# Moving four pieces of a two-layer trunk's first layer: parameter loads, token matrices, the gate's way up, and four weight splits

## The chip, the cores and the metric

One Trainium2 chip, one core of it. The metric is device time in microseconds of one execution. TensorE (PE) multiplies, VectorE (DVE), ScalarE (ACT) and GpSimd (POOL) do the rest, SyncE (SP) issues DMAs. Each engine runs its own list of instructions in order and waits on semaphores.

## What is computed

A trunk of two residual layers over x (1 x 256 x 1024, float32), each followed by a squared-ReLU MLP (1024 to 4096 and back). Layer 1 mixes tokens with sparse attention and isn't touched. Layer 0, where the change lies, is RWKV-7 time mixing:

```python
dx = shift(x) - x
xr, xw, xk, xv, xa, xg = (x + dx * mu[i] for i in range(6))
r, k, v = xr @ W_r, xk @ W_k, xv @ W_v
w_log = -softplus(-(w0 + tanh(xw @ w1) @ w2)) - 0.5
decay = exp(-exp(w_log))
a = sigmoid(a0 + (xa @ a1) @ a2)
g = sigmoid(xg @ g1) @ g2                      # the gate; g1 is 1024 x 160, g2 is 160 x 1024
kk = heads(k * k_k) / norm;  k = k * (1 + (a - 1) * k_a)
S_t = S_{t-1} diag(w_t) + (S_{t-1} (-kk_t)) (kk_t a_t)^T + v_t k_t^T;  y_t = S_t r_t
out = ((groupnorm(y) + bonus) * g) @ w_out     # bonus = sum(r k r_k) v, a head at a time
```

## The kernel before

Activations lie features first: 128 partitions x 8 feature tiles (FT) x 256 tokens. Weights of the big products stream in units of 128 x 1024 (four contraction tiles x 256 output columns) through a ring of four slots. Each unit is loaded into `raw` by SP, split by ACT into a rounded high part `whi` (`split`, L1076) and by DVE into the rest `wlo` (`rest`, L1468); `ahead(u)` does so for unit u + 4. TensorE adds three products a tile: whi by xh, whi by xl, wlo by xh (L450 to L452). `linear8` runs a projection: four groups of two units, with `between(g)` called behind a group and `after_unit(u)` behind a unit. Everything is ordered by hand: each engine's list, with semaphores.

*Front.* SP loads x by tokens, constants, 14 small pieces of parameters (`prow`), `spread`, then the weight units. ACT sums squares of x (L1097) and takes the root; DVE takes its reciprocal (L1483) and scales the identity and the shift matrix by it (`tokmat`, L1488). TensorE transposes the parameters (L472), which DVE copies to `par` (L1479) ahead of the reciprocal; then it multiplies x by `tokmat` (L483 to L485), which normalizes, transposes and takes the token difference in one. ACT takes that out to `xd` two features a call (`xd_out`), DVE mixes (`mix_pair`, L1496), ACT rounds (`upper`, L1125), DVE makes the rest (`lower`, L1505).

*Projections r, k, v.* Between the groups of v lie small products: `between_v(0)` spreads the inverse norms of kk (16 contraction rows, L594), `between_v(1)` is the gate's way up (`g_up`, L575 with 128 rows and L576 with 32), `between_v(2)` the pair sums for the bonus (L603). ACT computes E1, E2, E3 (exponentials of the running decay), DVE the factors AR and BK, and behind v TensorE transposes BK (`b_k`, L613) and V (L625). ACT and DVE copy these to BKT and UV; POOL multiplies the bonus by V (L2035).

*Inversion.* Two pairs of two sets of triangular 64 x 64 matrices are inverted (L658, L667), each opened by ACT's copy `Lr`, two masks by POOL, and DVE's mask, transpose and sum (L1686 to L1691).

*Recurrence.* Four chunks c of 64 tokens (NCH). TensorE's list in a chunk: `xs_state`, `y_state`, `gn_mean(c-1)`, u (L805), `gn_var(c-1)`, state (L815), `y_values`, `xs_values(c+1)`, `gn_spread(c-1)` (L755). DVE's: copies XS (L1739), `gn_scale(c-2)`, copy UV, the state's update, `gn_rstd(c-1)` (L1720, L1722), which `gn_spread` waits for. ACT's: XS, squares and copy for the mean, UV, `gn_sqrt`, the two y copies (L1296), `gn_upper(c-2)`. POOL applies the gate and makes `yl`. Then comes the output projection o0; its first four units are split right behind v's last.

Of the kernel before, what the change touches and what calls it, by code (L numbers as in the profile page):

```python
# [15 lines left out]
HD = 64  # L16
H = D // HD
C = 64
NCH = T // C
# [83 lines left out]
def rwkv_nsa_trunk(nc, t, out):  # L103
# [56 lines left out]
    lup_g1 = place("lup_g1", [LG - P, D], off(9, 4 * D))  # L160
    hg0 = place("hg0", [P, T], misc + 128)
    hg1 = place("hg1", [LG - P, T], misc + 128 + 4 * T)
# [145 lines left out]
    def sem(name):  # L308
        if name not in sems:
            sems[name] = ctx.enter_context(nc.semaphore(name))  # L310
        return sems[name]

    with ctx:
# [10 lines left out]
        def _(sp):  # L324
# [4 lines left out]
            pr = sem("par_in")  # L329
            for i, n in enumerate(["mix_norm", "mlp_norm"]):  # L330
                sp.dma_start(prow[16 * i:16 * i + 16, 0, :], t[n].rearrange("a (k p) -> (a k) p", p=P)).then_inc(pr, 16)
            sp.dma_start(prow[32:80, 0, :], t["rwkv_mu"][0].rearrange("a (k p) -> (a k) p", p=P)).then_inc(pr, 16)
            for i, n in enumerate(["rwkv_w0", "rwkv_a0", "rwkv_k_k", "rwkv_k_a"]):
                sp.dma_start(prow[80 + 8 * i:88 + 8 * i, 0, :], t[n][0].rearrange("(k p) -> k p", p=P)).then_inc(pr, 16)
            sp.dma_start(prow[112:120, 0, :], t["rwkv_r_k"][0].rearrange("(k a) n -> k (a n)", a=2)).then_inc(pr, 16)
            sp.dma_start(prow[120:128, 0, :], t["rwkv_ln_w"][0].rearrange("(k p) -> k p", p=P)).then_inc(pr, 16)
            sp.dma_start(prow[0:8, 1, :], t["rwkv_ln_b"][0].rearrange("(k p) -> k p", p=P)).then_inc(pr, 16)
            for a in range(2):
                sp.dma_start(prow[8:9, 1, a * HD:(a + 1) * HD], t["nsa_q_norm"]).then_inc(pr, 16)
                sp.dma_start(prow[9:12, 1, a * HD:(a + 1) * HD], t["nsa_k_norm"][0]).then_inc(pr, 16)  # L340
# [25 lines left out]
            sp.dma_start(lup_g1[:, :], t["rwkv_g2"][0][P:LG, :]).then_inc(lo, 16)  # L366
# [52 lines left out]
        def _(pe):  # L419
# [146 lines left out]
            def g_up():  # L566

                pe.wait_ge(sem("kkn_used"), 1)
                for g in range(4):
                    if g >= 2:  # L570
                        pe.wait_ge(sem("up_out"), 16 + g - 1)
                    for m in range(2):
                        c0 = (2 * g + m) * P
                        o = ps[:, 4 + 2 * (g % 2) + m, 0:T]
                        mm(o, lup_g0[:, c0:c0 + P], hg0[:, :], start=True, stop=False)  # L575
                        last = mm(o, lup_g1[:, c0:c0 + P], hg1[:, :], start=False, stop=True)  # L576
                    last.then_inc(sem("up_pe"), 1)
# [9 lines left out]
            def between_v(g):  # L587

                if g == 0:
                    pe.wait_ge(sem("spread_in"), 16)  # L590
                    pe.wait_ge(sem("lora_act"), 3)
                    pe.wait_ge(sem("kk_inv"), 1)
                    for k in range(FT):
                        last = mm(ps[:, 4 + k // 2, (k % 2) * T:(k % 2 + 1) * T], hspread(k), kkr[:, 1, :],  # L594
                                  start=True, stop=True)
                    last.then_inc(sem("kk_pe"), 1)
                if g == 1:
                    g_up()
                if g == 2:
                    pe.wait_ge(sem("rk"), 1)  # L600
                    pe.wait_ge(sem("up_out"), 20)
                    for j in range(4):
                        last = mm(ps[:, 4 + j, :], cc("pair"), t11[:, 2 * j:2 * j + 2, :], start=True, stop=True)  # L603
                    last.then_inc(sem("kk_pe"), 1)

            linear8("v", xh[0], xl[0], "v", between_v)


# [8 lines left out]
            pe.wait_ge(sem("bk_ready"), 2)  # L617
            pe.wait_ge(sem("rk_copied"), 1)
            b_k(0)
            b_k(1)  # L620
# [437 lines left out]
        def _(act):  # L1058
# [33 lines left out]

            act.wait_ge(sem("eps_set"), 3)
# [43 lines left out]
            upper("r", 0, 0)  # L1137
            xd_out(2)
            upper("r", 0, 1)
            xd_out(3)  # L1140
            split(1)
# [60 lines left out]
            A(hg1[:, :], ps[0:LG - P, 5, 0:T], ACT.Sigmoid).then_inc(sem("lora_act"), 1)  # L1202
# [3 lines left out]
            act.wait_ge(sem("cs_ready"), 1)  # L1206
            A(E1[:, :, :], CSm[:, :, :], ACT.Exp, scale=-DECAY).then_inc(sem("e1_ready"), 1)
# [3 lines left out]
            act.wait_ge(sem("ex_ready"), 1)  # L1211
            A(E2[:, :, :], CSm[:, :, :], ACT.Exp, scale=DECAY).then_inc(sem("e2_ready"), 1)
            A(E3[:, :, :], Sg[:, :, :], ACT.Exp, scale=-DECAY).then_inc(sem("e3_ready"), 1)
            evac_of("v", V, 1)
            ahead(U0["v"] + 2)
            ahead(U0["v"] + 3)
            for g in range(4):
                act.wait_ge(sem("up_pe"), FT + g + 1)
                b = 4 + 2 * (g % 2)
                A(Gt[:, 2 * g:2 * g + 2, :], ps[:, b:b + 2, 0:T], ACT.Copy).then_inc(sem("up_out"), 1)  # L1220
            evac_of("v", V, 2)
            ahead(U0["v"] + 4)
            ahead(U0["v"] + 5)
            act.wait_ge(sem("kk_pe"), KK_PE["rk_sum"])
            A(t11[:, :, :].rearrange("p (b k) t -> p b (k t)", b=4), ps[:, 4:8, :], ACT.Copy).then_inc(sem("rk_copied"), 1)
            evac_of("v", V, 3)
            ahead(U0["v"] + 6)
            ahead(U0["v"] + 7)
# [7 lines left out]
            bkt_copy(0)  # L1236

# [44 lines left out]
            for c in range(NCH):  # L1282
                for half in range(2):
                    act.wait_ge(sem(f"xs_pe{half}"), c + 1)
                    if c == 0:
                        act.wait_ge(sem("u_zero"), 1)
                    A(XS[half][0:HD, :, 0, :], quarter(ps[0:HD, 3 * half, 0:GW]), ACT.Copy).then_inc(sem(f"x_even{half}"), 1)
                if c:
                    gn_square(c - 1)
                act.wait_ge(sem("u_pe0"), c + 1)  # L1290
                A(UV[0:HD, c, 0:512], ps[0:HD, 1, :], ACT.Copy).then_inc(sem("u_sb0"), 1)
                if c:
                    gn_sqrt(c - 1)
# [159 lines left out]
        def _(dve):  # L1453
# [24 lines left out]
            dve.wait_ge(sem("par_t"), 1)  # L1478
            v.tensor_copy(par[:, 0:NPAR], ps[:, 7, 0:NPAR]).then_inc(sem("par_r"), 1)  # L1479
            dve.wait_ge(sem("par_r"), 1)  # L1480

# [8 lines left out]
            v.tensor_scalar(lastcol[:, :], tokc[:, P:P + 2], tiny[:, 6:7], None, ALU.mult).then_inc(sem("tok_ready"), 1)  # L1490

# [50 lines left out]
            for n in range(4):  # L1542
                dve.wait_ge(sem("xd_out"), 2 * n + 2)
                mix_pair(0, mixd[0], n)
                if n == 2:
                    rest(1, 2)
                if n:
                    lower("r", 0, n - 1)
            lower("r", 0, 3)
# [58 lines left out]
            for k in range(FT):  # L1608
# [4 lines left out]
            dve.wait_ge(sem("kk_pe"), KK_PE["kk_spread"])  # L1613
            v.tensor_tensor(KK[:, :, :].rearrange("p (b k) t -> p b (k t)", b=4), KK[:, :, :].rearrange("p (b k) t -> p b (k t)", b=4),
                            ps[:, 4:8, :], ALU.mult).then_inc(sem("kkn_used"), 1)
# [7 lines left out]
            dve.wait_ge(sem("kkn_used"), 1)  # L1623
            v.tensor_tensor(Ai[:, :, :], KK[:, :, :], Ai[:, :, :], ALU.mult).then_inc(sem("b_ready"), 1)
            dve.wait_ge(sem("up_out"), 20)
            dve.wait_ge(sem("e2_ready"), 1)
            step(v.tensor_tensor(arv(BK, 1), ch(K), ch(E2), ALU.mult))
            dve.wait_ge(sem("b_ready"), 1)
            v.tensor_tensor(arv(BK, 0), ch(Ai), ch(E2), ALU.mult).then_inc(sem("bk_ready"), 1)
            ahead2("v", 2)  # L1630
            dve.wait_ge(sem("e1_ready"), 1)
            step(v.tensor_tensor(arv(AR, 1), ch(R), ch(E1), ALU.mult))
            step(v.tensor_copy(PC[:, :, :], E1[:, :, :].rearrange("p k (c n) -> p k c n", n=C)[:, :, :, C - 1]))
            settle()
            dve.sem_inc(sem("rk_done"), 1)
            dve.sem_inc(sem("bk_ready"), 1)
            dve.sem_inc(sem("ar_ready"), 1)
            dve.wait_ge(sem("e3_ready"), 1)
# [3 lines left out]
            ahead2("v", 4)  # L1642
            ahead2("v", 6)
            dve.wait_ge(sem("bk_ready"), 2)
# [89 lines left out]
            for c in range(NCH):  # L1734
# [385 lines left out]
```

## Time and profile before

| | us |
|---|---|
| median of three runs | 859.94 |
| lowest and highest | 853.4, 860.27 |
| the profiled execution | 860.52 |
| its span, first to last instruction | 858.6 |
| mean granted TensorE clock | 0.959 |

| engine | busy us | share of the span |
|---|---|---|
| TensorE | 801.3 | 93% |
| DVE | 540.4 | 63% |
| ACT | 378.6 | 44% |
| POOL | 71.0 | 8% |

The median is that of whole executions; the profile is of one of them, and its times count from its first instruction. In the lists of the trace the first number is the start in us, the second the busy time. PEclk is the share of the full TensorE clock that was granted; full speed is 2.4 GHz, 0.50 is 1.2 GHz. A float32 product leaves two records in the trace, one of the split kind one.

### The profile page before, as it was taken

The numbers are of one execution on the slowest core, as the hardware profiler recorded it, in microseconds if no ns is written. First come the engines' busy times: TensorE is split into PE (matmuls) and PEld (weight loads), VectorE is DVE, ScalarE is ACT, GpSimd is POOL, SyncE is SP. The second block draws the span as 40 slices with busy tenths as digits, with TensorE's granted clock in tenths as the row PEclk, the third lists the DMA queues.
The fourth block names the chain that finished last, engine by engine and source line by source line (L and its number), as shares of the span: only waits on it lengthen the run. The fifth ranks groups of instructions, "written<-read, shape, count | busy, mean of one in ns | idle before, by whom it ended". The sixth has DMA issues, their size and how long they took to land.

```text
span 858.6 us, 18088 instructions
## 1 busy us (share of the span) xinstructions
PE 801.3 (93%) x7567; PEld 735.3 (86%) x7567; DVE 540.4 (63%) x780; ACT 378.6 (44%) x581; POOL 71.0 (8%) x48
## 2 busy tenths in 40 slices
PE   5899997988886999999999999978989999999997
PEld 4898776888765999999999988864549999999997
DVE  2785868667443687775455784567955877764441
ACT  4666625121332544443444434356755544443331
POOL 0000003164031000000000010003420000000000
PEclk9999889789997999999999999968999999999999
DMA  7753114000000579866565534310003565666551
GB/s 243 221 173 124 50 50 141 10 3 3 3 2 2 171 209 232 227 191 207 178 192 177 170 121 120 119 57 2 1 2 113 170 188 173 189 198 194 174 171 49
DMA packets 109995, 107.62 MB, mean 125 GB/s; under 512 B 7224, under 2 KB 108992, under 8 KB 109936
## 3 DMA queue, kind: packets, MB, share of 16 engines
q1 hardware_dynamic: 109936, 106.77, 41.5%
q8 instruction: 45, 0.74, 0.4%
q14 instruction: 14, 0.11, 0.0%
HBM read 105.71 MB, written 1.05 MB: 124 GB/s over the span
## 4 chain that ended last, share of the span: by engine, by line
PE 84%; DVE 10%; issue 2%; ACT 2%; SPq 1%; POOL 0%; DMA 0%; ACTq 0%; DVEq 0%
PE ps L450 21%; PE ps L452 21%; PE ps L451 20%; PE ps L667 4%; DVE SB L1970 1%; DVE nmx L1974 1%; PE ps L1022 1%; DVE Gs L1660 1%; PE ps L805 1%; PE ps L562 1%; PE ps L887 1%; PE ps L1005 1%; PE ps L483 1%; PE ps L948 1%; ACT SB L1416 1%
## 5 line engine op out<-in xcount | busy, mean ns | idle before, releaser
L1468 DVE TENSOR_TENSOR wlo<-raw,whi 128x1024 fp32r<-128x1024 f32 x188 | 228.5, 1240 | 112.3 <-ACT whi L1076 110.9
L450 PE MATMUL ps<-xh,whi 128*128 128x256 f32 x896 | 257.1, 287 | 2.1 <-DVE xl L1505 2.1
L452 PE MATMUL ps<-xh,wlo 128*128 128x256 f32 x896 | 255.3, 285 | 0.0
L451 PE MATMUL ps<-xl,whi 128*128 128x256 f32 x896 | 255.1, 285 | 0.0
L1076 ACT ACTIVATE whi<-raw 128x1024 fp32r<-128x1024 f32 x124 | 130.0, 1058 | 154.6 <-PE ps L452 149.8
L450 PEld LDWEIGHTS ps<-xh,whi 128*128 128x128 f32 x896 | 171.5, 191 | 7.7 <-issue 6.8
L451 PEld LDWEIGHTS ps<-xl,whi 128*128 128x128 f32 x896 | 171.1, 191 | 0.3 <-issue 0.2
L452 PEld LDWEIGHTS ps<-xh,wlo 128*128 128x128 f32 x896 | 171.2, 191 | 0.0
L452 PE MATMUL ps<-hh,wlo 128*128 128x256 f32 x512 | 145.0, 283 | 0.0
L451 PE MATMUL ps<-hl,whi 128*128 128x256 f32 x512 | 144.7, 283 | 0.0
L450 PE MATMUL ps<-hh,whi 128*128 128x256 f32 x512 | 144.0, 281 | 0.0
L1318 ACT ACTIVATE whi<-raw 128x1024 fp32r<-128x1024 f32 x64 | 67.9, 1061 | 87.4 <-PE ps L452 78.1
L450 PEld LDWEIGHTS ps<-hh,whi 128*128 128x128 f32 x512 | 96.8, 189 | 0.0
L452 PEld LDWEIGHTS ps<-hh,wlo 128*128 128x128 f32 x512 | 96.6, 189 | 0.0
L451 PEld LDWEIGHTS ps<-hl,whi 128*128 128x128 f32 x512 | 96.3, 188 | 0.0
L1797 DVE SCALAR_TENSOR_TENSOR rl<-ps,ri 128x512 f32<-128x512 f32 x32 | 22.1, 692 | 38.8 <-PE ps L452 38.3
L667 PE MATMUL ps<-DP,LT 64*64 64x64 f32 x1024 | 37.0, 238 | 5.7 <-DVE DP L1691 4.7
L667 PEld LDWEIGHTS ps<-DP,LT 64*64 64x64 f32 x1024 | 35.7, 153 | 6.7 <-DVE DP L1691 5.5
L1509 DVE TENSOR_TENSOR h<-h,ps 128x512 f32<-128x512 f32 x16 | 11.0, 688 | 37.6 <-PE ps L452 34.7
L1416 ACT ACTIVATE SB<-SB,nmx 128x128 f32<-128x128 f32 (+1 forms) x64 | 28.2, 443 | 12.1 <-DVE nmx L1976 12.0
L2085 POOL TENSOR_TENSOR SB<-SB,cof 128x512 f32<-128x512 f32 (+1 forms) x16 | 23.5, 1467 | 111.5 <-DVE cof L1988 111.5
L1248 ACT ACTIVATE DP<-ps 128x512 f32<-128x512 f32 x16 | 9.6, 597 | 37.2 <-PE ps L667 37.2
(288 smaller groups left out, 1044.0 us busy)
## 6 DMA issues: line engine op xcount, KB each, us to landing
raw<-in_mlp_w SPq DMA_DIRECT2D x128, 512.0 KB, 4.5
raw<-in_rwkv_w_in SPq DMA_DIRECT2D x24, 512.0 KB, 4.2
raw<-in_nsa_w_in SPq DMA_DIRECT2D x20, 512.0 KB, 3.7
raw<-in_rwkv_w_out SPq DMA_DIRECT2D x8, 512.0 KB, 3.9
raw<-in_nsa_w_out SPq DMA_DIRECT2D x8, 512.0 KB, 3.9
cw<-in_nsa_cmp_w SPq DMA_DIRECT2D x4, 512.0 KB, 8.6
xtok<-in_x SPq DMA_DIRECT2D x2, 512.0 KB, 4.0
out<-otok SPq DMA_DIRECT2D x2, 512.0 KB, 2.8
```

What stands on the lines that cost most here:

```text
L450: mm(o, wh, hi[:, kk, :], start=(kk == 0), stop=False)
L451: mm(o, wh, lo[:, kk, :], start=False, stop=False)
L452: last = mm(o, wl, hi[:, kk, :], start=False, stop=(kk == ktiles - 1))
L667: last = mm(ps[at(e), bank, p * C:(p + 1) * C], lhs[s][at(e), p, :], DP[s][at(e), p, which, :], start=True, stop=True)
L1076: A(whi[:, s, :], raw[:, s, :], ACT.Copy).then_inc(hi_ready, 1)
L1248: A(dst, ps[:, bank, :].rearrange("p (k n) -> p k n", n=C), ACT.Copy).then_inc(sem(f"inv_act{s}"), 1)
L1318: A(whi[:, 2 * gg + j, :], raw[:, 2 * gg + j, :], ACT.Copy).then_inc(hi_ready, 1)
L1416: o = A(SB[n % 4][:, i, 0:w], SB[n % 4][:, i, 0:w], ACT.Exp, bias=nmx[:, n % 4, i:i + 1], accum_out=den[:, q, b, hd:hd + 1])
L1468: v.tensor_tensor(wlo[:, slot, :], raw[:, slot, :], whi[:, slot, :].bitcast(f32), ALU.subtract)\
L1509: v.tensor_tensor(h[:, 2 * g:2 * g + 2, :], h[:, 2 * g:2 * g + 2, :], ps[:, 2 * (g % 2):2 * (g % 2) + 2, 0:T], ALU.add).then_inc(ev_dve, 1)
L1797: v.scalar_tensor_tensor(rl[:, gg, :, :], ps[:, 2 * gg:2 * gg + 2, 0:T], 0.0, normal(2), ALU.max, ALU.mult)\
L2085: g.tensor_tensor(x, x, cof[:, q, b, 4 * j:4 * j + 4].unsqueeze(2).broadcast_to([P, 4, w]), ALU.mult)\
```

## The change

- The 14 loads of parameters leave SP's queue and stand at the head of ACT's, ahead of its first activation.
- DVE makes the token matrices first and copies the parameters behind them.
- The gate's second piece (32 contraction rows) is widened to 128 rows: `lup_g1` and `hg1` get 128 partitions and POOL fills them with zeros first. SP waits for that before it loads `lup_g1`.
- `g_up` moves from behind v's group 1 to behind group 0, the spread of the inverse norms from group 0 to group 1. The pair sums now wait for `kkn_used` too.
- The transposes of BK move from behind v to behind its unit 6.
- ACT: the second unit's split ahead of two `xd_out`; Exp and gate copies in the new order; `bkt_copy(0)` ahead of the last copy of V.
- DVE: R's and K's factors first, KK's behind them; splits of v's last units in between.
- The splits of o0's first four units leave both ACT and DVE behind v, and come one a chunk into the recurrence.

```diff
-    lup_g1 = place("lup_g1", [LG - P, D], off(9, 4 * D))
+    lup_g1 = place("lup_g1", [P, D], off(9, 4 * D))
-    hg1 = place("hg1", [LG - P, T], misc + 128 + 4 * T)
+    hg1 = place("hg1", [P, T], misc + 128 + 4 * T)
@@ SP, behind tokc: 14 loads of prow on sp leave
-            pr = sem("par_in")
-            for i, n in enumerate(["mix_norm", "mlp_norm"]):
-                sp.dma_start(prow[16 * i:16 * i + 16, 0, :], t[n].rearrange("a (k p) -> (a k) p", p=P)).then_inc(pr, 16)
...
@@ SP
-            sp.dma_start(lup_g1[:, :], t["rwkv_g2"][0][P:LG, :]).then_inc(lo, 16)
+            sp.wait_ge(sem("g_zero"), 2)
+            sp.dma_start(lup_g1[0:LG - P, :], t["rwkv_g2"][0][P:LG, :]).then_inc(lo, 16)
@@ TensorE
             def g_up():
 
-                pe.wait_ge(sem("kkn_used"), 1)
+                pe.wait_ge(sem("lora_act"), 3)
+                pe.wait_ge(sem("kk_root"), 1)
@@
                 if g == 0:
+                    g_up()
+                if g == 1:
                     pe.wait_ge(sem("spread_in"), 16)
-                    pe.wait_ge(sem("lora_act"), 3)
+                    pe.wait_ge(sem("up_out"), 20)
                     pe.wait_ge(sem("kk_inv"), 1)
...
-                if g == 1:
-                    g_up()
                 if g == 2:
                     pe.wait_ge(sem("rk"), 1)
-                    pe.wait_ge(sem("up_out"), 20)
+                    pe.wait_ge(sem("kkn_used"), 1)
...
-            linear8("v", xh[0], xl[0], "v", between_v)
...
-            pe.wait_ge(sem("bk_ready"), 2)
-            pe.wait_ge(sem("rk_copied"), 1)
-            b_k(0)
-            b_k(1)
+            def after_v(u):
+                if u == 6:
+                    pe.wait_ge(sem("bk_ready"), 2)
+                    pe.wait_ge(sem("rk_copied"), 1)
+                    b_k(0)
+                    b_k(1)
+
+            linear8("v", xh[0], xl[0], "v", between_v, after_unit=after_v)
@@ ACT
+            pr = sem("par_in")
+            for i, n in enumerate(["mix_norm", "mlp_norm"]):
+                act.dma_start(prow[16 * i:16 * i + 16, 0, :], t[n].rearrange("a (k p) -> (a k) p", p=P)).then_inc(pr, 16)
...
             act.wait_ge(sem("eps_set"), 3)
@@
             upper("r", 0, 0)
+            split(1)
             xd_out(2)
             upper("r", 0, 1)
             xd_out(3)
-            split(1)
@@
-            A(hg1[:, :], ps[0:LG - P, 5, 0:T], ACT.Sigmoid).then_inc(sem("lora_act"), 1)
+            act.wait_ge(sem("g_zero"), 2)
+            A(hg1[0:LG - P, :], ps[0:LG - P, 5, 0:T], ACT.Sigmoid).then_inc(sem("lora_act"), 1)
...
-            act.wait_ge(sem("cs_ready"), 1)
-            A(E1[:, :, :], CSm[:, :, :], ACT.Exp, scale=-DECAY).then_inc(sem("e1_ready"), 1)
             evac_of("v", V, 0)
             ahead(U0["v"])
             ahead(U0["v"] + 1)
-            act.wait_ge(sem("ex_ready"), 1)
-            A(E2[:, :, :], CSm[:, :, :], ACT.Exp, scale=DECAY).then_inc(sem("e2_ready"), 1)
-            A(E3[:, :, :], Sg[:, :, :], ACT.Exp, scale=-DECAY).then_inc(sem("e3_ready"), 1)
-            evac_of("v", V, 1)
-            ahead(U0["v"] + 2)
-            ahead(U0["v"] + 3)
             for g in range(4):
                 act.wait_ge(sem("up_pe"), FT + g + 1)
                 b = 4 + 2 * (g % 2)
                 A(Gt[:, 2 * g:2 * g + 2, :], ps[:, b:b + 2, 0:T], ACT.Copy).then_inc(sem("up_out"), 1)
+            act.wait_ge(sem("ex_ready"), 1)
+            act.wait_ge(sem("cs_ready"), 1)
+            A(E1[:, :, :], CSm[:, :, :], ACT.Exp, scale=-DECAY).then_inc(sem("e1_ready"), 1)
+            A(E2[:, :, :], CSm[:, :, :], ACT.Exp, scale=DECAY).then_inc(sem("e2_ready"), 1)
+            evac_of("v", V, 1)
+            ahead(U0["v"] + 2)
+            A(E3[:, :, :], Sg[:, :, :], ACT.Exp, scale=-DECAY).then_inc(sem("e3_ready"), 1)
+            ahead(U0["v"] + 3)
             evac_of("v", V, 2)
-            ahead(U0["v"] + 4)
-            ahead(U0["v"] + 5)
...
-            evac_of("v", V, 3)
-            ahead(U0["v"] + 6)
-            ahead(U0["v"] + 7)
...
             bkt_copy(0)
+            evac_of("v", V, 3)
@@ ACT, recurrence, behind the two y copies of chunk c
+                ahead(U0["v"] + 4 + c)
                 if c >= 2:
                     gn_upper(c - 2)
@@ DVE
-            dve.wait_ge(sem("par_t"), 1)
-            v.tensor_copy(par[:, 0:NPAR], ps[:, 7, 0:NPAR]).then_inc(sem("par_r"), 1)
-            dve.wait_ge(sem("par_r"), 1)
-
             dve.wait_ge(sem("tok_root"), 1)
...
             v.tensor_scalar(lastcol[:, :], tokc[:, P:P + 2], tiny[:, 6:7], None, ALU.mult).then_inc(sem("tok_ready"), 1)
+            dve.wait_ge(sem("par_t"), 1)
+            v.tensor_copy(par[:, 0:NPAR], ps[:, 7, 0:NPAR]).then_inc(sem("par_r"), 1)
+            dve.wait_ge(sem("par_r"), 1)
@@
                 mix_pair(0, mixd[0], n)
-                if n == 2:
-                    rest(1, 2)
                 if n:
                     lower("r", 0, n - 1)
+                if n == 1:
+                    rest(1, 2)
@@ DVE, order behind K's update (after): 2 splits, r k r_k (rk), then
+            step(v.tensor_tensor(arv(AR, 1), ch(R), ch(E1), ALU.mult))
+            step(v.tensor_copy(PC[:, :, :], E1[:, :, :].rearrange("p k (c n) -> p k c n", n=C)[:, :, :, C - 1]))
+            dve.wait_ge(sem("e2_ready"), 1)
+            step(v.tensor_tensor(arv(BK, 1), ch(K), ch(E2), ALU.mult))
...
+            ahead(U0["v"] + 2)
             dve.wait_ge(sem("kk_pe"), KK_PE["kk_spread"])
...
+            ahead(U0["v"] + 3)
             dve.wait_ge(sem("b_ready"), 1)
             v.tensor_tensor(arv(BK, 0), ch(Ai), ch(E2), ALU.mult).then_inc(sem("bk_ready"), 1)
...
-            ahead2("v", 4)
-            ahead2("v", 6)
-            dve.wait_ge(sem("bk_ready"), 2)
@@ DVE, recurrence
                 v.tensor_copy(UV[0:HD, c, 512:1024], ps[0:HD, 4, :]).then_inc(sem("u_sb1"), 1)
+                if c == NCH - 1:
+                    ahead(U0["v"] + 4 + c)
                 if c < NCH - 1:
...
+                    ahead(U0["v"] + 4 + c)
                 if c:
                     gn_rstd(c - 1)
@@ POOL, at its head
+            g.memset(lup_g1[:, :], 0.0).then_inc(sem("g_zero"), 1)
+            g.memset(hg1[:, :], 0.0).then_inc(sem("g_zero"), 1)
```

## Rows read from the trace of the kernel before

**Rows 1.** The page: the chain's shares by engine, and the group of DVE's splits

```profile
PE 84%; DVE 10%; issue 2%; ACT 2%; SPq 1%; POOL 0%; DMA 0%; ACTq 0%; DVEq 0%
...
L1468 DVE TENSOR_TENSOR wlo<-raw,whi 128x1024 fp32r<-128x1024 f32 x188 | 228.5, 1240 | 112.3 <-ACT whi L1076 110.9
```

**Rows 2.** Windows: us, PE, PEld, DVE, ACT, POOL busy (instructions), PEclk, DMA

```profile
27.00:30.40 3.40, 3.40 (x19) 3.40 (x18) 3.00 (x5) 2.52 (x3) 0.00 (x0) 0.54 0.89 268
...
30.40:95.00 64.60, 64.60 (x488) 55.69 (x487) 50.64 (x75) 40.42 (x62) 0.00 (x0) 1.00 0.43 131
...
104.00:107.00 3.00, 3.00 (x12) 2.35 (x11) 1.84 (x1) 2.25 (x2) 0.00 (x0) 0.50 0.00 0
...
123.00:126.00 3.00, 3.00 (x16) 3.00 (x16) 2.67 (x2) 0.30 (x1) 0.00 (x0) 0.50 0.00 0
```

**Rows 3.** Timeline of SP's queue: start us, us, what

```profile
2.61 0.43 SPq L331 DMA_DIRECT2D prow<-in_mix_norm  x1
...
7.31 0.25 SPq L340 DMA_DIRECT2D prow<-in_nsa_k_norm  x1
```

**Rows 4.** Timeline of the front: start us, us, what [idle before <-releaser]

```profile
0.74 1.28 ACT L1094 ACT_TABLE_LOAD   x1 [0.74 <-PEq L2101]
...
4.36 1.06 ACT L1097 ACTIVATE sqs<-xtok 128x1024 f32<-128x1024 f32 x1 [2.12 <-DMA xtok<-in_x]
...
6.83 0.29 ACT L1099 ACTIVATE tiny<-tiny 128x2 f32<-128x2 f32 x1
...
9.69 0.17 DVE L1483 RECIPROCAL tiny<-tiny 128x2 f32<-128x2 f32 x1
...
11.05 1.19 PE L483 MATMUL ps<-tokmat,xtok 128*128 128x256 f32 x2 [1.74 <-DVE lastcol L1490]
```

**Rows 5.** Timeline of the front, second unit and first gap

```profile
23.43 1.05 ACT L1076 ACTIVATE whi<-raw 128x1024 fp32r<-128x1024 f32 x1
...
26.48 0.36 PE L450 MATMUL ps<-xh,whi 128*128 128x256 f32 x1 [2.15 <-DVE xl L1505]
```

**Rows 6.** Chain that ended last, in order of time, value projection

```profile
83.57 7.22 PE ps L562 x32
...
100.13 4.92 PE ps L594 x16
...
113.27 0.62 PE ps L576 x2
```

**Rows 7.** Timeline behind the value projection

```profile
139.11 1.91 PE L613 MATMUL ps<-cst,BK 128*128 128x128 f32 x16
...
140.08 4.55 POOL L2035 TENSOR_TENSOR t<-t,V 128x2048 f32<-128x2048 f32 x1 [139.63 <-ACT V L1149]
...
140.89 5.96 DVE L1468 TENSOR_TENSOR wlo<-raw,whi 128x1024 fp32r<-128x1024 f32 x2 [3.33 <-ACT whi L1076]
...
150.64 1.65 PE L658 MATMUL ps<-BK,AR 64*64 64x64 f32 x26 [4.55 <-DVE UV L1650]
```

**Rows 8.** Chain that ended last, the inversion's two pairs

```profile
155.76 10.72 PE ps L667 x288
...
178.66 0.70 DVE LT L1686
...
184.43 10.10 PE ps L667 x288
```

**Rows 9.** Timeline of the recurrence

```profile
230.19 0.85 ACT L1296 ACTIVATE AR<-ps 128x256 f32<-128x256 f32 x2 [1.22 <-PE ps L790]
...
232.40 1.12 PE L755 MATMUL ps<-rsb,spread 16*128 16x512 f32 x2 [0.60 <-DVE rsb L1722]
...
243.00 1.77 DVE L1722 TENSOR_TENSOR rsb<-rst,spread 16x512 f32<-16x512 f32 x1
...
254.07 0.85 ACT L1296 ACTIVATE AR<-ps 128x256 f32<-128x256 f32 x2 [0.32 <-PE ps L790]
...
255.09 1.12 PE L755 MATMUL ps<-rsb,spread 16*128 16x512 f32 x2 [0.60 <-DVE rsb L1722]
```

More of the change, by code:

```diff
@@ L328, in _ @@
             sp.dma_start(tokc[:, :], t["consts"][:, kept:]).then_inc(sem("cst_in"), 16)
-            pr = sem("par_in")
-            for i, n in enumerate(["mix_norm", "mlp_norm"]):
-                sp.dma_start(prow[16 * i:16 * i + 16, 0, :], t[n].rearrange("a (k p) -> (a k) p", p=P)).then_inc(pr, 16)
[L332 to L340, printed above, removed]
             sp.dma_start(spread[:, :], t["spread"]).then_inc(sem("spread_in"), 16)
@@ L1090, in evac8 @@
                         after_first()
+            pr = sem("par_in")
+            for i, n in enumerate(["mix_norm", "mlp_norm"]):
+                act.dma_start(prow[16 * i:16 * i + 16, 0, :], t[n].rearrange("a (k p) -> (a k) p", p=P)).then_inc(pr, 16)
+            act.dma_start(prow[32:80, 0, :], t["rwkv_mu"][0].rearrange("a (k p) -> (a k) p", p=P)).then_inc(pr, 16)
+            for i, n in enumerate(["rwkv_w0", "rwkv_a0", "rwkv_k_k", "rwkv_k_a"]):
+                act.dma_start(prow[80 + 8 * i:88 + 8 * i, 0, :], t[n][0].rearrange("(k p) -> k p", p=P)).then_inc(pr, 16)
+            act.dma_start(prow[112:120, 0, :], t["rwkv_r_k"][0].rearrange("(k a) n -> k (a n)", a=2)).then_inc(pr, 16)
+            act.dma_start(prow[120:128, 0, :], t["rwkv_ln_w"][0].rearrange("(k p) -> k p", p=P)).then_inc(pr, 16)
+            act.dma_start(prow[0:8, 1, :], t["rwkv_ln_b"][0].rearrange("(k p) -> k p", p=P)).then_inc(pr, 16)
+            for a in range(2):
+                act.dma_start(prow[8:9, 1, a * HD:(a + 1) * HD], t["nsa_q_norm"]).then_inc(pr, 16)
+                act.dma_start(prow[9:12, 1, a * HD:(a + 1) * HD], t["nsa_k_norm"][0]).then_inc(pr, 16)
             act.wait_ge(sem("eps_set"), 3)
@@ L1612, in _ @@
             settle()
-            dve.wait_ge(sem("kk_pe"), KK_PE["kk_spread"])
-            v.tensor_tensor(KK[:, :, :].rearrange("p (b k) t -> p b (k t)", b=4), KK[:, :, :].rearrange("p (b k) t -> p b (k t)", b=4),
-                            ps[:, 4:8, :], ALU.mult).then_inc(sem("kkn_used"), 1)
             ahead2("v", 0)
@@ L1622, in _ @@
             arv = lambda x, n: x[:, :, :, n, :].rearrange("p k c n -> p (k c) n")
-            dve.wait_ge(sem("kkn_used"), 1)
-            v.tensor_tensor(Ai[:, :, :], KK[:, :, :], Ai[:, :, :], ALU.mult).then_inc(sem("b_ready"), 1)
             dve.wait_ge(sem("up_out"), 20)
[L1626 to L1630, printed above, removed]
             dve.wait_ge(sem("e1_ready"), 1)
@@ L1637, in _ @@
             dve.sem_inc(sem("ar_ready"), 1)
+            ahead(U0["v"] + 2)
+            dve.wait_ge(sem("kk_pe"), KK_PE["kk_spread"])
+            v.tensor_tensor(KK[:, :, :].rearrange("p (b k) t -> p b (k t)", b=4), KK[:, :, :].rearrange("p (b k) t -> p b (k t)", b=4),
+                            ps[:, 4:8, :], ALU.mult).then_inc(sem("kkn_used"), 1)
+            dve.wait_ge(sem("kkn_used"), 1)
+            v.tensor_tensor(Ai[:, :, :], KK[:, :, :], Ai[:, :, :], ALU.mult).then_inc(sem("b_ready"), 1)
+            ahead(U0["v"] + 3)
+            dve.wait_ge(sem("b_ready"), 1)
+            v.tensor_tensor(arv(BK, 0), ch(Ai), ch(E2), ALU.mult).then_inc(sem("bk_ready"), 1)
             dve.wait_ge(sem("e3_ready"), 1)
```

## The prediction

> **What bounds the kernel now.** First the page: the chain that ended last is 84% TensorE [rows 1], so a change pays where TensorE waits, or computes for longer than it must. TensorE never pauses from 30.4 to 95.0 us [rows 2]: what is won before 30 us is handed on by that stretch, if ACT and DVE keep up. Then the timeline, stage by stage. Four places matter here.
>
> *Front.* SP issues 14 parameter loads from 2.61 to 7.56 us, and the queue does other loads only after them [rows 3]. The squares of x start at 4.36 us, their root is there at 7.12, and the token products start at 11.05 [rows 4]. Later TensorE waits 2.15 us for xl, queued on DVE behind the second unit's split, which waited for ACT's half of it (23.43 to 24.48) [rows 5]. After that gap 27.0 to 30.4 runs at a granted clock of 0.54, about the 1.2 GHz level [rows 2].
>
> *Value projection.* The gate's way up puts 128 contraction rows and 32 rows in turn on the array; two records take 0.62 us (16 such rows, one shown), where the way down with 128 rows needs 7.22 us for 32 records, 0.45 for two [rows 6]. Behind two sparse pieces the clock falls: 104 to 107 is at 0.50 (inside the spread with 16 rows, which took 4.92 us), and 123 to 126 at 0.50 behind the gate [rows 2, 6].
>
> *Entry into the recurrence.* POOL's bonus product runs from 140.08 to 144.63. Two of DVE's low splits take 5.96 us beside it, and the copy to UV behind them releases TensorE after 4.55 us of idle [rows 7]. The second group's inversion starts only at 155.76 [rows 8]. The same opening in pair 1 of the inversion, with no late copy, takes from 178.66 to 184.43 [rows 8].
>
> *Recurrence.* TensorE waits for the row scales of DVE's gn_rstd at 232.40 and 255.09, just 0.60 us after its last work [rows 9].
>
> **Front, part by part.** The 14 issues go ahead of everything on ACT. At SP's price (7.56 - 2.61 = 4.95) they end at 0.75 + 4.95 = 5.70. Behind them on ACT are the table load (1.28), the small root (about 0.2) and the squares with their root (7.12 - 4.36 = 2.76) [rows 4]: ready at 9.94, not 7.12. Of these 2.8 us, 2.5 are covered, since DVE's reciprocal waited for the parameters until 9.69 [rows 4], a wait that now stands behind the token matrices. Remaining cost: 0.3. Landing, transpose and copy of the parameters took 9.69 - 7.56 = 2.1 us after the last issue; TensorE's part of it now comes by 7.8 and is hidden up to 11.3, when the token products ask. Moved splits: the second unit's ACT half now comes before xd of features 4 and 5 and costs those about one copy; DVE's half is done before xl(1) is asked for, so the 2.15 us go. With no gap I take its slow stretch away too: 3.4 us at half clock, 1.7. Front: 2.15 + 1.7 - 0.3 = **3.5 earlier**. Raw tiles are issued 5 us earlier and can't be late; the POOL memsets are 128x1024 and 128x256 at a time when POOL has nothing, and SP reaches the wait for them after some twenty issues.
>
> **Value projection.** One shape: 16 x (0.62 - 0.45) = 2.7, between 0 (the bubbles stay) and 3.2. Without bubbles I take the slow stretch behind the gate away, 1.7. I keep the one in the 16-row spread, as that piece is the same (if it goes: 3.4 more, for 6.8 us at half). The transposes of BK (1.91 for 16) move in front of the last unit [rows 7]; they had run beside the V copy that POOL waits for, and now delay it: -1.9. A new wait to check is bk_ready ahead of the last unit. ACT's gate copies end 0.6 us behind the gate; table load (1.28) and E1 (1.9) follow, so DVE starts R times E1 at +3.9. Up to the second bk_ready it has five products of 2.3, two splits of 1.2 and the copy to PC, 14.1: bk_ready at +18. TensorE needs it only after v group 1, spread, group 2, pair sums and unit 6: 5.8 + 3.5 + 5.8 + 3.4 + 2.9 = 21.4. Hidden with 3 us to spare. Sum: 2.7 + 1.7 - 1.9 = **2.5 earlier** at the V copy.
>
> **Entry.** The two splits of the projection's first units are gone from in front of DVE's copies, and two on ACT. Counted from the bonus's start: it ends at +4.55; Lr copy 0.6 and passing on, +5.3; then the opening as in pair 1, 5.77 (POOL's masks contending with DVE, as there): +11.1. Before, 155.76 - 140.08 = 15.7. So **4.6 earlier**, between 3.5 (if the clock stays low longer than the 10.72 us of the first run of 288 products) and 5.2 (if it goes as in pair 1, 10.10) [rows 8].
>
> **Recurrence.** Four splits come in, one a chunk: ACT's 1.05 after the y copies, DVE's 1.2 behind it (mean 1240 ns) [rows 1, 5]. The y copies have a row a chunk, two of the four shown [rows 9]. Queued behind DVE's, which waits for ACT's, is gn_rstd, and for that TensorE waits in order, with the next chunk's xs_state behind it.
> - Chunk 0: no gn_rstd. Done at 222.13 + 1.05 + 1.2 = 224.4; the odd copies end at 225.3, TensorE asks for the first at 225.6. Cost 0.
> - Chunk 1: y copies end 231.04 [rows 9]; ACT to 232.1, DVE to 233.3, gn_rstd 1.25, TensorE at 234.6 instead of 232.40: 2.2.
> - Chunk 2: y copies end 242.37; DVE done 244.65, gn_rstd and some of POOL's yl product beside it. Before, that product already stretched the scale to 1.77 us, up to 244.77 [rows 9]; now to 246.1: 1.3.
> - Chunk 3: the split is ahead of gn_rstd(2), behind ACT's of this chunk: y copies end 254.92, ACT 255.95, DVE 257.2, scales 258.4, TensorE 258.5 instead of 255.09 [rows 9]: 3.4.
>
> Sum 6.9, all exposed. TensorE's gaps grow from 0.6 us to about 2.8 and 4.0; the gap of 2.15 in the front was followed by a slow stretch, so I add 1.2 (after chunk 1) and 1.5 (in the tail): 2.7, between 0 and 3.5. **9.6 later.** The loads of the projection's last units wait for these splits; the last is issued near 258 and lands before the projection asks (267.6).
>
> **Sum.** -3.5 - 2.5 - 4.6 + 9.6 = -1.0. The profiled execution took 860.5 (span 858.6 plus 1.9 around it), 0.6 over the median of the three; -1.0 gives 859.5 for it and **858.9** against the median of 859.94.
>
> The front's 3.5 rests on issue time alone: SP's 4.95 us for 14 issues [rows 3]. A rule of the Trainium skill limits what a second issuing engine can bring: "DMA: Bandwidth & Descriptors", section "Issuing engines are not separate DMA queues", says that it saves only the issuer's own time, since the transfers run on the same engines. By it nothing would be gained in transfer time, and I count none; that two issuers don't hinder each other no row here shows (rival 1).
>
> **Rivals.** (1) *The two queues' issues hold each other up.* If ACT's 14 alternate with SP's, they end at 0.75 + 2 x 4.95 = 10.65, TensorE's start is 5 us later: 858.9 + 5.0 = 863.9, slower than before. It decides from 1.0 us added to ACT's issues on. For it: nothing here ever issued from two engines at once. Against: ACT's are 24 KB and less, and rows 3 show 0.25 to 0.4 us each. Chance 0.17. (2) *The moved splits are covered after all and the clock is kind*: gn_rstd isn't late, and the spread's slow stretch goes: 859.94 - 10.6 - 3.4 = 845.9; with only one of the two, 849.3 (splits hidden) or, with the stretches in spread and recurrence all gone, 852.8. Against: rows 9 show how tight the scales are. Chance 0.20. (3) *The shape isn't the cause of the gate's bubbles*: 2.7 and 1.7 stay lost: 858.9 + 4.4 = 863.3. Chance 0.08. (4) *Recurrence dearer*: long gaps keep the clock low through chunks 2 and 3, two stretches more of 3.4: 858.9 + 3.4 = 862.3. Chance 0.10. The forecast, small gains eaten by the recurrence, has 0.45.
>
> **Range.** From 850.5 (the clock's part of rival 2, with some of the splits covered) to 865 (rival 1 and a little of 4). The likeliest case alone: 855 to 862. A measurement of this kernel can tell about 1% (8.6 us) from no change. Faster by more needs most of rival 2: 0.19. Slower by more needs rivals 1, 3 and 4 together: 0.06. Within 1%: 0.75.
>
> **What would show it.** Right: token products start within 0.5 us of 11.05 and r's first group has no gap; two gate records in 0.45 us; first inversion products some 10 us earlier than 155.8; TensorE idle before the spreads of the row scales of 2.8, 1.7 and 4 us with DVE's split in front. Wrong: ACT's issues taking over 0.5 us each; a gap inside the value projection (bk_ready late); in the recurrence, DVE's splits ending before TensorE's own work; slow-clock stretches elsewhere than named.

## The result, and the profile after

The changed kernel takes 859.7 us (median of 20 executions, 856.69 to 861.52), the kernel before 854.95 (20, 851.8 to 860.29). The ratio is 1.0047, 95% interval 1.003 to 1.0065: **slower, by 2.6 to 5.6 us**, where 1.0 us faster was forecast. The move is far below 1%, but the runs tell it from none, and its sign is the wrong one.

The three executions seen before the forecast (853.4, 859.94, 860.27) had a median 5 us above that of twenty, and the profiled one (860.52) lay at the upper end. The kernel before was therefore profiled once more (e0 below, span 848.9). The table measures each stage between the starts of the same instructions: ACT's first copy of R, its square of KK, POOL's bonus, the first u product (L805, L795 after), and ACT's last yh.

| stage, us | before, first profile | before, second profile | changed |
|---|---|---|---|
| start to the first copy of R | 32.6 | 32.1 | 28.7 |
| to the square of KK | 53.7 | 53.7 | 53.7 |
| to the bonus (value projection) | 53.8 | 49.2 | 49.2 |
| to the first u (inversion) | 77.3 | 76.9 | 71.9 |
| to the last yh (recurrence) | 48.7 | 49.6 | 64.0 |
| rest of the span | 592.5 | 587.4 | 590.1 |
| span | 858.6 | 848.9 | 857.6 |

The front and the entry (the start of the inversion's stage) gained what was forecast. The recurrence lost half as much again as forecast: 14.3 us against the second profile, for 9.6. The rest of the span, which the change doesn't touch, moves by 5 us between the two profiles of one program, and so does the value projection.

Timeline of the changed kernel, front: start us, us, what [idle before <-releaser]; first ACT's last parameter issue.

```profile
5.74 0.30 ACTq L1094 DMA_DIRECT2D prow<-in_nsa_k_norm  x1
...
9.82 0.29 ACT L1101 ACTIVATE tiny<-tiny 128x2 f32<-128x2 f32 x1
...
10.97 0.45 PE L461 MATMUL ps<-cst,prow 128*128 128x128 f32 x1 [10.97 <-DMA prow<-in_nsa_k_norm]
...
11.55 1.22 PE L472 MATMUL ps<-tokmat,xtok 128*128 128x256 f32 x2
...
28.65 0.60 ACT L1151 ACTIVATE R<-ps 128x512 f32<-128x512 f32 x1 [1.52 <-PE ps L441]
```

ACT's issues ended at 6.04, for 5.70 forecast; the root came at 10.11, for 9.94. The parameters, however, landed 4.9 us after their last issue, among SP's weight loads [rows 4 had all of landing, transpose and copy in 2.1]. TensorE transposed them at 10.97, and the token products followed without a pause at 11.55. The last of DVE's token factors (`lastcol`) was ready at 11.36, and before the change the products started 0.15 us behind it, so hardly anything was lost here; but nothing was to spare either. In e2 below, with the same order, the parameters came at 11.37 and the products at 11.95, about 0.5 us later than they could have. The first copy of R is 3.9 us earlier than in the first profile, 3.5 earlier than in the second.

Chain of the changed kernel: the gate, and the first run of inversion products; between them the timeline's bonus.

```profile
96.66 0.43 PE ps L566 x2
```

```profile
131.57 4.53 POOL L2038 TENSOR_TENSOR t<-t,V 128x2048 f32<-128x2048 f32 x1 [129.63 <-ACT V L1151]
```

```profile
142.54 10.29 PE ps L657 x288
```

Two records of the gate's second piece take 0.43 us, for 0.62 in [rows 6]. From the bonus to the inversion's products it is 11.0 us, for 15.7 in [rows 7, 8].

Timeline of the changed kernel, chunks 1 and 3: DVE's split, then the spread that waited.

```profile
219.40 1.22 DVE L1468 TENSOR_TENSOR wlo<-raw,whi 128x1024 fp32r<-128x1024 f32 x1 [1.03 <-ACT whi L1066]
220.54 0.53 DVE L1717 RECIPROCAL rst<-rst 16x64 f32<-16x64 f32 x1
221.11 0.68 DVE L1719 TENSOR_TENSOR rsb<-rst,spread 16x512 f32<-16x512 f32 x1
221.84 2.07 PE L745 MATMUL ps<-rsb,spread 16*128 16x512 f32 x2 [2.73 <-DVE rsb L1719]
...
250.93 1.23 DVE L1468 TENSOR_TENSOR wlo<-raw,whi 128x1024 fp32r<-128x1024 f32 x1 [2.77 <-ACT whi L1066]
...
253.87 2.07 PE L745 MATMUL ps<-rsb,spread 16*128 16x512 f32 x2 [4.35 <-DVE rsb L1719]
```

The order on DVE is to be seen: split, reciprocal, row scales, and only then the spread. DVE first stood idle for 1.03 us, until ACT had done its half (218.25 to 219.30), so the place costs 1.03 + 1.22 in chunk 1. TensorE waits 2.73, 3.23 and 4.35 us in chunks 1, 2 and 3, for 0.60, 1.69 and 0.60 before [rows 9 show two of these; chunk 2 before is in the trace of the kernel before, here below]. The spread itself takes 2.07 us, for 1.12: it runs at half the clock.

```profile
244.82 1.23 PE L755 MATMUL ps<-rsb,spread 16*128 16x512 f32 x2 [1.69 <-DVE rsb L1722]
```

Windows of the changed kernel (us, PE, PEld, DVE, ACT, POOL busy with instructions, PEclk, DMA share, GB/s).

```profile
203.50:268.00 64.50, 48.05 (x662) 35.20 (x656) 24.52 (x39) 20.58 (x40) 12.47 (x9) 0.74 0.11 34
...
221.50:228.30 6.80, 6.46 (x68) 4.49 (x68) 1.83 (x4) 0.75 (x2) 1.15 (x1) 0.51 0.24 80
238.60:245.40 6.80, 6.80 (x68) 4.00 (x67) 1.54 (x3) 0.76 (x2) 1.97 (x2) 0.52 0.13 45
252.30:268.00 15.70, 8.07 (x22) 3.12 (x22) 5.46 (x8) 2.44 (x5) 4.76 (x4) 0.50 0.10 33
```

Each of the three waits goes with a stretch at 1.2 GHz, the last one through the whole tail and on until 272.5. A slow tail by itself is nothing new: the second profile of the kernel before has one of 10.2 us, and e6 below one of 17, both without the long waits.

### The profile page after: what moved, and what is told of

It is laid out like the page before. It is cut to its first block, busy times and chain, and to the rows that moved or that the text cites. A ratio compares the mean times of both kernels' runs of the same rounds, so it can differ in the third digit from the quotient of the medians.

```text
span 857.6 us, 18092 instructions
## 1 busy us (share of the span) xinstructions
PE 797.7 (93%) x7567; PEld 733.6 (86%) x7567; DVE 537.6 (63%) x780; ACT 378.2 (44%) x581; POOL 74.0 (9%) x50
## 4 chain that ended last, share of the span: by engine, by line
PE 85%; DVE 10%; ACT 2%; issue 1%; ACTq 1%; DMA 1%; POOL 1%; DVEq 0%; POOLq 0%
PE ps L439 21%; PE ps L441 20%; PE ps L440 20%; PE ps L657 4%; DVE SB L1970 1%; DVE nmx L1974 1%; DVE Gs L1657 1%; PE ps L795 1%; PE ps L745 1%; PE ps L1012 1%; PE ps L551 1%; PE ps L877 1%; PE ps L938 1%; PE ps L735 1%; DVE wlo L1468 1%
## 5 line engine op out<-in xcount | busy, mean ns | idle before, releaser
L1468 DVE TENSOR_TENSOR wlo<-raw,whi 128x1024 fp32r<-128x1024 f32 x188 | 225.3, 1222 | 110.4 <-ACT whi L1066 108.7
L439 PEld LDWEIGHTS ps<-xh,whi 128*128 128x128 f32 x896 | 169.7, 189 | 5.0 <-issue 4.1
L440 PEld LDWEIGHTS ps<-xl,whi 128*128 128x128 f32 x896 | 169.3, 189 | 0.3 <-issue 0.2
L441 PEld LDWEIGHTS ps<-xh,wlo 128*128 128x128 f32 x896 | 169.4, 189 | 0.0
```

What stands on the lines that cost most here:

```text
L439: mm(o, wh, hi[:, kk, :], start=(kk == 0), stop=False)
L440: mm(o, wh, lo[:, kk, :], start=False, stop=False)
L441: last = mm(o, wl, hi[:, kk, :], start=False, stop=(kk == ktiles - 1))
L1468: v.tensor_tensor(wlo[:, slot, :], raw[:, slot, :], whi[:, slot, :].bitcast(f32), ALU.subtract)\
```

## The experiments

**e0: the kernel before, profiled again.** No edit.

> The kernel before, unchanged, profiled again. The forecast took its terms from a profile of 860.5 us, 5.6 over the median of twenty (854.95). If the clock alone makes that spread: a ratio of 1.000, and a profile near 855 with fewer or shorter stretches at 1.2 GHz than the first profile's nine, at the same durations of every other engine. If the spread has another cause (loads, an engine): the same stretches, and other waits.

854.09 us (849.86 to 860.46), ratio 0.9998 (0.9968 to 1.0028). Windows of this second profile, and of the first over the same two stages:

```profile
80.00:135.00 55.00, 55.00 (x331) 41.92 (x330) 41.51 (x44) 27.09 (x31) 0.00 (x1) 1.00 0.25 75
...
211.90:262.00 50.10, 39.78 (x660) 31.07 (x656) 20.35 (x35) 16.76 (x36) 11.37 (x9) 0.91 0.01 2
```

```profile
84.00:140.00 56.00, 56.00 (x304) 42.83 (x304) 41.12 (x44) 25.68 (x29) 0.00 (x0) 0.91 0.22 68
```

In the value projection TensorE was busy without a pause in both; the second profile had the full clock all through, the first 0.91. Of the 9.7 us between the spans 4.6 lie in that stage. So the slow stretches of [rows 2] at 104 and 123 us are there in one execution and gone in the next, of one and the same program.

**e1: the kernel before with the recurrence's splits alone.** On both engines the four splits behind v go, and come back a chunk each:

```diff
# ACT, behind the y copies of chunk c
+                ahead(U0["v"] + 4 + c)
# DVE, ahead of gn_rstd (in the last chunk behind the copy UV)
+                    ahead(U0["v"] + 4 + c)
                 if c:
                     gn_rstd(c - 1)
```

> The kernel before with one part of the change: the four splits of the projection's first units leave their place behind v and come one a chunk into the recurrence. Theory A (their place in the recurrence costs 6.9 us of exposed waits and some 8 of low clock): entry 4.7 us earlier, recurrence 12 to 15 longer, 862 to 865 against 855. Rival B (the recurrence of the changed kernel is long because of the clock's phase, the splits add little): 850 to 852. The forecast's own terms: -4.6 + 9.6, 860.

863.47 us (861.85 to 867.64), ratio 1.0129 (1.0088 to 1.017). Theory A. The inversion's stage shrank to 73.8 us, the recurrence grew to 61.3. TensorE's three waits are again 2.73, 3.23 and 4.35 us. The growth of 11.7 over the second profile is these waits' 7.4 and 4.3 of clock, so the clock's part isn't a fixed size.

This run's front, which its edit doesn't touch, shows one thing more. The gap ahead of xl is there, but no slow stretch follows it, and the first copy of R comes at 29.98, for 32.56 and 32.13 in the two profiles before:

```profile
25.22 0.36 PE L450 MATMUL ps<-xh,whi 128*128 128x256 f32 x1 [2.15 <-DVE xl L1502]
```

```profile
25.20:30.00 4.80, 4.78 (x38) 4.65 (x39) 4.40 (x7) 2.55 (x4) 0.00 (x0) 1.00 0.89 256
```

**e2: the changed kernel with these splits back behind v.**

```diff
             evac_of("v", V, 2)
+            ahead(U0["v"] + 4)
+            ahead(U0["v"] + 5)
...
             evac_of("v", V, 3)
+            ahead(U0["v"] + 6)
+            ahead(U0["v"] + 7)
# DVE
+            ahead2("v", 4)
+            ahead2("v", 6)
             dve.wait_ge(sem("bkT"), 2)
```

> The changed kernel with these four splits back behind v, on ACT and DVE, everything else as changed. Theory A: gives back the entry's 4.7 us and wins 12 to 15 in the recurrence, 850 to 853. Rival B: 864. In the profile, by A, the wait of the row scales' spread falls from 2.7, 3.2 and 4.4 us to below 1.7, and fewer stretches at 1.2 GHz between 200 and 270.

850.99 us (847.35 to 852.88), ratio 0.9946 (0.9917 to 0.9976). The rest of the change without this part is faster than the kernel before; recurrence 49.7 us, inversion 78.4. With e1 this is a square of four: the part costs 8.0 us on the kernel before (855.49 in these runs to 863.47) and 8.7 on the rest of the change (850.99 to 859.7). By the ratios it is 11.0 (7.5 to 14.5) and 8.6. It is the cause of the sign.

**e3: the same splits at another place of the same stretch.**

```diff
# ACT, ahead of the loop over chunks
+            for c in range(NCH):
+                ahead(U0["v"] + 4 + c)
# DVE, every chunk
+                ahead(U0["v"] + 4 + c)
                 dve.wait_ge(sem("u_pe1"), c + 1)
```

> The changed kernel with the four splits at another place of the same stretch: ACT's all ahead of chunk 0, where it idles 10 us; DVE's one a chunk between the copies XS and UV, where it idles 2.4 to 4.2 us waiting for TensorE. Theory A (what costs is the place ahead of gn_rstd, not the work): 845 to 848, recurrence as before the change (50 us) and the entry's gain kept. Rival B: 859 to 860. A rival C (work of DVE and ACT anywhere in the recurrence costs, through POOL's port or the clock): 852 to 856.

845.84 us (843.98 to 849.1), ratio 0.9911 (0.9881 to 0.9941). Timeline of its chunk 1:

```profile
220.38 1.12 PE L745 MATMUL ps<-rsb,spread 16*128 16x512 f32 x2 [0.60 <-DVE rsb L1720]
```

The same work in the same 50 us costs nothing there: the wait is back at 0.60, and the entry's gain stays. That rules out rival C.

**e6: the changed kernel with DVE's split one place later.**

```diff
-                if c == NCH - 1:
-                    ahead(U0["v"] + 4 + c)
...
-                    ahead(U0["v"] + 4 + c)
                 if c:
                     gn_rstd(c - 1)
+                ahead(U0["v"] + 4 + c)
```

> The changed kernel with DVE's split of each chunk one place later, behind gn_rstd in place of ahead of it; ACT's stays. If the order of these two on DVE is the cause: chunk 1 and 3 lose their waits (1.9 and 3.8 us), DVE's split then runs while TensorE works on the next chunk's products and may hold up the copies XS by under 1 us a chunk: 847 to 851. Rival (any split of 1.2 us in the chunk is on the path): 857 to 860.

845.53 us (844.23 to 846.68), ratio 0.9884 (0.985 to 0.9918). Swapping two neighbours on DVE is worth 14 us. ACT's splits stayed, so ACT's half cost something only through DVE's wait for it. Chunk 1:

```profile
219.56 0.68 DVE L1719 TENSOR_TENSOR rsb<-rst,spread 16x512 f32<-16x512 f32 x1
220.17 1.20 DVE L1468 TENSOR_TENSOR wlo<-raw,whi 128x1024 fp32r<-128x1024 f32 x1
220.29 1.12 PE L745 MATMUL ps<-rsb,spread 16*128 16x512 f32 x2 [0.61 <-DVE rsb L1719]
```

DVE's split now runs beside the spread and the products behind it, and is done before the copies XS are asked for (222.07). All three waits are back at 0.60 us. The tail stays at 1.2 GHz even so (window below, TensorE busy for 6.18 of 13.6 us), and the recurrence takes 50.2 us: the same as before the change.

```profile
242.40:256.00 13.60, 6.18 (x21) 2.83 (x22) 5.04 (x8) 2.54 (x5) 5.33 (x4) 0.50 0.12 39
```

**e7: filler in the waits.** The changed kernel; the products' results are overwritten by the spread, so what is computed stays the same.

```diff
                 if c:
+                    pe.wait_ge(sem("y_std"), c)
+                    for _ in range(4 if c == NCH - 1 else 3):
+                        mm(ps[:, 7, :], cc("center"), AR[:, :, c - 1, 0, :], start=True, stop=True)
                     gn_spread(c - 1)
```

> The changed kernel with filler on TensorE where it waits for the row scales: 3, 3 and 4 products of 128 x 512 float32 (about 0.9 us each) into the bank that the spread then overwrites, in chunks 1, 2 and 3. No other engine's work changes, and the exposed waits of 7.4 us over the kernel before stay. Theory A1 (the other 7 us of the recurrence's 14.3 are TensorE's low clock behind these waits): 853 to 856 against 859.7, with far fewer than 33 us at 1.2 GHz between 203 and 268. Rival A2 (they come from POOL's port and ACT's order): 860 to 862.

852.1 us (849.52 to 857.29), ratio 0.9961 (0.9932 to 0.999), against 859.7. Windows and timeline:

```profile
205.60:261.00 55.40, 46.19 (x684) 32.11 (x678) 24.91 (x40) 20.68 (x40) 12.49 (x9) 0.97 0.12 39
```

```profile
220.00 2.84 PE L815 MATMUL ps<-AR,cst 128*128 128x512 f32 x6
...
222.07 0.68 DVE L1722 TENSOR_TENSOR rsb<-rst,spread 16x512 f32<-16x512 f32 x1
222.80 1.12 PE L745 MATMUL ps<-rsb,spread 16*128 16x512 f32 x2
```

TensorE's own work of the chunk ends at 220.07, 2.73 us before the spread, exactly as in the changed kernel, and TensorE does useless work until 222.84; yet the clock over the recurrence is 0.97 for 0.74, the spread takes 1.12 for 2.07, and the kernel is 7.6 us faster (7.4 by the ratios). This measures the clock's part by itself, and rules out A2. In the profile the recurrence takes 54.6 us, for 64.0. That is 9.4 less, where the changed kernel has 6.9 of clock over the kernel before: filler also takes away low clock that the kernel before has in this stage (0.91 in e0).

**e4: e3 with the gate's second piece narrow.** `lup_g1` and `hg1` back to 32 partitions, without the zero fill and its two waits.

> The fast variant (splits in the wait, 845.84) with the gate's second piece back to 32 contraction rows, without the zero fill and its waits. By the forecast (16 changes of shape cost 0.17 each): 2.7 us longer, 4.4 with a stretch at low clock behind it: 848.5 to 850.2, and two of the gate's records in 0.62 us. Rival (the shape isn't the cause): within 1 us of 845.8.

849.6 us (848.42 to 855.22), ratio 0.9934 (0.9905 to 0.9962): by the medians 3.8 us over e3, by the two ratios to the kernel before, which ran beside each, 2.0. The intervals of the two ratios overlap. Its chain:

```profile
100.06 0.62 PE ps L565 x2
```

The bubbles are back. The bonus starts 3.5 us later (135.62 for 132.10), 3.2 of it in the value projection (52.4 for 49.2). The shape is the cause of that; what it is worth at the end isn't settled closer than 2.0 to 3.8.

**e5: e3 with the second unit's split late.** `split(1)` back behind `xd_out(3)`, `rest(1, 2)` back to n = 2.

> The fast variant (845.84) with only the second unit's split back in its old place, on ACT and on DVE; the parameters stay on ACT's queue. If that split alone carries the front's 3.9 us: 848 to 850, with TensorE's gap of some 2.1 us before 27 us. Rival (the parameters' new queue and the token matrices carry it): 845 to 846.5.

851.43 us (846.92 to 853.82), ratio 0.9933 (0.9908 to 0.9957): by the medians 5.6 us over e3, by the ratios 1.9. The gap is back as in [rows 5], and the first copy of R comes 3.7 us later (32.88 for 29.18):

```profile
26.82 0.36 PE L439 MATMUL ps<-xh,whi 128*128 128x256 f32 x1 [2.15 <-DVE xl L1505]
```

The split's place alone carries the shift between these two kernels: 2.15 us of gap, and a slow stretch behind it (27.2 to 30.6), which e1 with the same gap doesn't have. What that is worth at the end lies between 1.9 and 5.6 us, and isn't settled closer: the intervals of the two ratios overlap, and the kernel before, against which the ratios go, is itself scattered.

**e8: e6 with the parameters back on SP's queue** and their copy ahead of the token matrices.

> The variant with DVE's split behind gn_rstd (845.53), with the 14 parameter loads back on SP's queue and DVE's copy of the parameters back ahead of the token matrices; the second unit's split stays early. By the forecast's terms the move of the loads brings nothing (a cost of 0.3 us): 845 to 846, token products starting at 11.0 in place of 11.5. Rival (SP's weight loads, 5 us earlier, carry part of the front's gain): 847 to 849, with a wait for a raw tile or for its split before 33 us.

845.46 us (845.0 to 846.5), ratio 0.9862 (0.9822 to 0.9901), against 845.53 for e6. The first two edits of the list bring nothing that these runs can tell. Token products start 0.4 us earlier than in the changed kernel:

```profile
11.14 1.19 PE L484 MATMUL ps<-tokmat,xtok 128*128 128x256 f32 x2 [1.74 <-DVE lastcol L1490]
```

**e9: e6 with filler in the tail.** Seven products into bank 1, which nobody reads then.

```diff
+            fill(1)
             gn_mean(NCH - 1)
             gn_var(NCH - 1)
+            fill(2)
             gn_spread(NCH - 1)
+            fill(4)
             pe.wait_ge(sem("yh_ready"), NCH)
```

> The variant with DVE's split behind gn_rstd (845.53), with seven filler products of 128 x 512 float32 on TensorE in the waits of the last chunk's tail (1 ahead of its mean, 2 ahead of its spread, 4 ahead of the projection), into a bank that nobody reads. In the profile of that variant TensorE runs at 1.2 GHz for 17 us from the tail into the projection. If filler keeps or brings back the clock there: 841 to 844. If the filler comes too late or lengthens the tail: 845 to 848.

843.33 us (841.59 to 843.9), ratio 0.9832 (0.9792 to 0.9872), the fastest of all: 2.2 us less than e6, and 2.1 less than e8, which ran beside it. Windows of e6 and of e9 over the recurrence:

```profile
204.00:256.00 52.00, 41.44 (x665) 31.48 (x662) 24.22 (x40) 20.67 (x40) 12.62 (x9) 0.84 0.14 42
```

```profile
204.00:256.00 52.00, 46.98 (x697) 34.42 (x692) 24.65 (x41) 20.67 (x40) 12.64 (x9) 0.97 0.13 42
```

## Why the prediction was wrong, point by point

- **Front: right in size, the credit for the clock less firm.** Forecast 3.5 earlier, measured 3.9 and 3.5 against the two profiles. e5 puts it on the second unit's split, e8 puts nothing on the parameters' queue. But 1.7 of the forecast was the slow stretch behind the gap. The kernel before has it in both profiles, and e5 too; e1 has the same gap and no such stretch. Rival 1 fell: with SP issuing at the same time, ACT's 14 issues took 5.3 us for SP's 4.95. Not foreseen was that their landing would take 4.9 us. The forecast hid the parameters' way with 3.5 us to spare (7.8 to 11.3), and nothing of that was left.
- **Value projection: the shape's part right, the credit for the clock wrong.** One shape saves 0.62 - 0.43 = 0.19 a change of shape, 3.0 for 16 (forecast 2.7), 3.2 in e4's stage; rival 3 fell. Moving BK's transposes gives 1.9 back by the list; no run tests it alone. bk_ready was in time: TensorE has no gap in that stage. But 1.7 of the forecast's 2.5 was a slow stretch of one profile, which e0's second profile doesn't have. The stage took 49.2 in both, the changed one with a slow stretch of 3.4 us in it.
- **Entry: right.** 4.6 forecast, 5.0 measured between bonus and first u.
- **Recurrence: the failed step.** The forecast was 9.6, as 6.9 exposed and 2.7 of clock. The first term stood: the waits grew by (2.73 + 3.23 + 4.35) - (0.60 + 1.69 + 0.60) = 7.4, chunk by chunk for the reason given. The mis-sized term is "I add 1.2 (after chunk 1) and 1.5 (in the tail): 2.7, between 0 and 3.5". The recurrence grew by 14.3 (64.0 for 49.6), so about 7 was clock, outside that range, and e7 gives 7.6 back by filler alone. I had looked at one short stretch behind each gap; what came was 6.8, 6.8 and 20.5 us at 1.2 GHz (252.0 to 272.5 the last). In the 15.7 us of the last that lie in the recurrence TensorE was busy for only 8.1, and the clock came up only in the projection. In e1 the same waits went with 4.3 us of clock: above the 3.5 there too.
- **The base, and luck.** The sum was made against one profile. Against that profile the number came true: 859.5 forecast for the profiled execution, 859.58 measured. That is luck. Stage by stage the changed kernel gained 3.9, 4.6 and 5.4 us, lost 15.3, and gained 2.4 in the rest of the span, which the change doesn't touch. A recurrence dearer by 5.7 than forecast was made up by the other terms, mostly by low clock that the first profile happened to have elsewhere. Against the second profile the same sum is -3.5 + 0.1 - 5.0 + 14.3 + 2.7 = +8.7. Twenty executions of each say +4.0 by the ratio. An estimate with the terms as read above (-3.9 for the front, -1.1 for shape less transposes, -5.0, +14.3), free of what the clock does elsewhere, is +4.3. It lies 5.3 above the forecast's -1.0: 4.7 for the recurrence, 1.4 for the value projection, and 0.8 back from front and entry.
- **Range and chances.** 859.7 lies in the range, and the move within 1% had 0.75. But the forecast called a sum of four terms of 3 to 10 us, known to some 3 us each, a gain of 1.0; its sign had no support. Rival 4 (recurrence dearer by low clock, at 862.3) was the right one, with 0.10 too low.
- **Rival 2** needed the splits covered. They can be, one place later on DVE, which the forecast didn't try: e6.

## What to carry to other kernels

Where an engine's list has room for work that nobody waits for yet, put it behind the instruction that another engine waits for, not ahead of it: the same 1.2 us split, with its own wait for ACT's half, cost 14 us in front of gn_rstd and nothing behind it. A new wait of TensorE can cost more than its length where sparse work follows: here 7.4 us of waits went with another 7 of low clock in one kernel, and with 4 in another. And before summing small terms, profile the base twice: what differs between two profiles of one program is no gain to count on.

## What the runs showed of the hardware

- One program's executions differ by where TensorE's clock falls: 849.86 to 860.46 us in twelve executions of the kernel before, with some 70 us at 1.2 GHz in the first profile (clock 0.959 over 858.6 us) and 51 in the second (0.970 over 848.9). e6 spread less (844.23 to 846.68 in six), e7 as much as 7.8 us in twelve. Why the sparse pieces of the value projection run at full clock in one execution and not in another stays open.
- A gap of 2.15 us in TensorE was followed by 3.4 us at 1.2 GHz in three profiles (both of the kernel before, and e5), and by none in e1. What decides it stays open.
- Filler products held the clock: 0.97 for 0.74 over the recurrence in e7, and 0.97 for 0.84 in e9, each with a gain.
- POOL's bonus product blocks a DVE split that reads two operands from SBUF (4.82 us for 1.21, in [rows 7]'s pair; the line at the end is the trace's of the kernel before, with minimum, median and maximum in ns), but not DVE's copies to UV out of PSUM, which took 1.2 us each beside POOL in the changed kernel (133.45 to 135.93), as without it in the kernel before (148.01 to 150.49). The Trainium skill, "SBUF — State Buffer", section "Who interferes with whom", has the first as an exclusive lock on a shared port pair, for a VectorE instruction with two SBUF inputs beside a GpSimd one that reads SBUF; the trace agrees: the split ended at 145.71, 1.1 us after POOL's end at 144.63.
- The 14 small loads landed 4.9 us after the last issue while SP's queue had its weight loads under way, for 1.1 us on SP's own queue ahead of them (7.56 to 8.66). That the big loads are the reason is argued, not tested. The transposes of the parameters waited for it, and in e2 the token products too.

```profile
L1468 DVE TENSOR_TENSOR wlo<-raw,whi x2: 1211/3016/4820, 140.9 to 145.6; 128x1024 fp32r<-128x1024 f32 x2
```
